# Four of twelve modulation chunks moved from the input projection into the first attention tile, with changes to row loads, hidden turns and the seams

## The chip, the cores and the metric

One core of a Trainium2 chip runs the whole program. The time is the device time of one execution in microseconds (us); the profile is one profiled execution of the same program. Engines: PE (TensorE), DVE (VectorE), ACT (ScalarE), POOL (GpSimd), and SP, which here only issues DMAs.

## The reference, cut to what matters

Two layers of a transformer block over 512 latent tokens and 256 context tokens, width 1024, all in float32. In the second layer only the latent tokens are carried on.

```python
for l in range(2):
    mod   = silu(c)     @ w_mod[l] + b_mod[l]      # (6144,) for the latent stream
    mod_c = silu(c_ctx) @ w_mod[l] + b_mod[l]      # (6144,) for the context stream
    sh1, sc1, g1, sh2, sc2, g2 = split(mod, 6)     # 1024 values each
    h = rms_norm(x, norm_mix) * (1 + sc1) + sh1
    u = h @ w_in[l]                                # 2400 columns: four mixers' q, k, v
    x = x + g1 * (concat(gqa, neighbourhood, diff, mla) @ w_out[l])
    h2 = rms_norm(x, norm_ffn) * (1 + sc2) + sh2
    x = x + g2 * (shared_expert(h2) + routed_experts(h2))   # 16 experts, top 2
out = rms_norm(x, final_norm)
```

The kernel computes `mod` in 12 chunks of 512 columns. Chunks 0 to 3 are sh1 and sc1, 4 and 5 are g1, 6 and 7 sh2, 8 and 9 sc2, 10 and 11 g2.

## The kernel before, in words

Every engine has its own program, written out by hand; semaphores (`s[...]`) tie them together, and each engine runs its instructions strictly in order. SP's program is a queue too: a wait in it holds back every DMA behind it. Each layer has four stages.

**Input projection** (`unit`, L1223 on). 24 units (4 column panels of `w_in` by 6 token tiles) run on PE, and between their halves the small `prep_round` transposes. `mod_product` (L1134) computes one modulation chunk: 32 products into one PSUM bank, of 128 columns each, four to a column group. Its weights are 2 MB, loaded by SP's `mod_load`. `MODS_AT` says behind the first half of which unit chunks 4 to 11 run in layer 0; `MODS_LATE` shifts them by two units in layer 1. DVE adds the bias rows in `mod_row`; `mod_gain` turns sc2 into the gain (chunks 8 and 9); SP's `mod_store` writes chunks 4 to 11 to the DRAM tensor `mod` once all are done.

**Attention**. `NS` = 10 steps for each tile of 128 query tokens, numbered n over all tiles. On PE a step is, in this order: `score` of the step; in the first tile, one or two `nb_unit`s (the last pieces of the projection, steps 0 to 5); the transposes of the step before for the first head (`product(.., 0)`, L1334); the product of an older step with the values (`values`, L1365, "the values between the two groups of transposes"); pieces of the output projection of the tile before (`out_piece`, L1382); and the transposes for the second head (`product(.., 1)`). Step 0 of tile 1 and some later ones use score operands (L1305) that SP has copied from one group of partitions to another: PE stands in `score` at n = 10 for `copies_in`.

After the bias loads SP's queue for the layer reads, in order (L699 to L712): wait for the last `nb_unit`; load `w_out` (4 MB, three DMAs, L700 and L701); load six broadcast vectors g1, sc2, sh2 of both streams from `mod` (0.5 MB each, L704); the eight partition copies (L711, L712); then the row loads and stores of the tiles (`att_rows`). The first of these is x of tile 0 (L722).

**Shared expert and routing**. `hs_load` brings back rows of h2 (L731), `s_turn` (L1440) transposes them, `s_gate`, `s_up`, `s_turn_hid` and `s_down` compute the shared expert, and the router's small products and DVE operations lie between them.

**Routed experts**, then the **seam**: the last block's rows come back through PE (`late_rows`, L1630), DVE adds them (`c_late`, `y_add`), and the next layer's `transpose_x` starts, or, in layer 1, the final norm and the stores.

Of the kernel before, what the change touches and what calls it, by code (L numbers as in the profile page):

```python
# [7 lines left out]
ALU = mybir.AluOpType  # L8
# [46 lines left out]
NB_IN_STEP = {0: [2], 1: [3], 2: [4], 3: [5], 4: [6], 5: [7]}  # L55
# [26 lines left out]
MODS_AT = {3: 4, 5: 5, 7: 6, 9: 7, 11: 8, 13: 9, 15: 10, 17: 11}  # L82
# [100 lines left out]
def program(nc, A, out):  # L183
# [15 lines left out]
    with ExitStack() as ctx:  # L199
# [74 lines left out]
        tmpA, tmpB = take(512), take(512)  # L274
        xt = [take(D) for _ in range(2)]
# [35 lines left out]
        def mod_norm_at(l, half):  # L311
# [13 lines left out]
        PTa, PTb, PTd = take(NTOK), take(NTOK + 2 * P), [take(NTOK), take(NTOK + P)]  # L325
        OT = [take(KT, P) for _ in range(2)]
        dO, dSq = take(P), take(P)
# [34 lines left out]
        mod_w = [[slot[0], slot[2], mod_w2, mod_w3] + [slot[2]] * (NMCH - 4),  # L362
                 mod_late + [slot[1], mod_w5, slot[2], mod_w5, slot[2], mod_w5] + [slot[2]] * (NMCH - 9)]
# [75 lines left out]
        copies_in = sem("copies_in")  # L439

        X_IN = ["x_in0", "x_in1"] + ["x_rest_in"] * (T - 2)
        NAMES = ["mod_w_in0", "mod_w_in1", "mod_w_in2", "mod_w_in3", "mod_w_in4", "mod_rows_in", "mod_mm", "mod_row", "mod_gain", "mod_stored",
# [91 lines left out]
        def nb_bank(n):  # L534

            return ubank[n] if n < NB_AHEAD else B7
# [45 lines left out]
        def _(sp):  # L582
            first = at["ident"][1]
            for l in range(DEPTH):
# [15 lines left out]
                def mod_store(l):  # L600
                    sp.wait_ge(s["mod_gain"], 2 * l + 2)
                    for r in range(2):
                        sp.dma_start(mod_d[l][r, 2 * D:6 * D].rearrange("(n q c) -> q n c", q=4, c=MODQ),
                                     mod_row0[r:P:32, 4:NMCH]).then_inc(s["mod_stored"], 16)
                    sp.wait_ge(s["mod_stored"], 32 * (l + 1))
# [33 lines left out]
                if l == 0:  # L639
# [24 lines left out]
                    for n in range(7, 10):  # L664
                        mod_load(0, n, n)
                    win_load(0, 3, 2 * T)
                    for n in range(10, NMCH):
                        mod_load(0, n, n)
                    win_load(0, 4, 3 * T)
                    mod_store(0)  # L670
                else:
# [5 lines left out]
                    for n in range(6, 9):  # L677
                        mod_load(1, n, n - 1)
                    win_load(1, 3, 2 * T)
                    mod_load(1, 9, 8)  # L680
                    for n in range(10, NMCH):
                        mod_load(1, n, n)
# [8 lines left out]
                for h in range(4):  # L691
                    for r2 in range(2):
# [146 lines left out]
                for t in range(nt):  # L839
# [11 lines left out]
                    if l == 0 and t == T - 1:  # L851

                        sp.wait_ge(late_y, late_tiles[0])
# [9 lines left out]
                for t in range(nt):  # L863
                    sp.wait_ge(s["c_x3"], gc(t) + 1)
                    sp.dma_start(dst(span(t * P, P)), x3[t]).then_inc(s[f"c_stored{t % 2}"], 16)
                for b in range(2):
                    sp.wait_ge(s[f"c_stored{b}"], 16 * (gend // 2))
# [3 lines left out]
        def _(act):  # L871
# [13 lines left out]
            for l in range(DEPTH):  # L885
# [55 lines left out]
                def evac_nb(n):  # L941

                    kind, i, c0, c1 = NB_UNITS[l][n]
                    act.wait_ge(s["u_mm"], UNIT0[l] + NTU + n + 1)
                    if n == 0:

                        act.wait_ge(s["mod_stored"], 32 * (l + 1))
# [185 lines left out]
        def _(pe):  # L1133
            pe.wait_ge(cs_ready, 3)  # L1134
            for l in range(DEPTH):
# [29 lines left out]
                def idle_products():  # L1165
# [1436 lines left out]
```

## Time and profile before

| | us |
|---|---|
| runs before: median, lowest, highest of 3 | 1645.83, 1645.29, 1653.87 |
| the profiled execution's own time | 1647.25 |
| its span in the profile | 1645.1 |
| PE busy in the span | 1572.1 (96%) |
| DVE, ACT, POOL busy | 837.5, 428.8, 196.8 |
| mean granted TensorE clock | 0.989 of full speed |

The span is the time from the first to the last instruction of the profile; 2.15 us of the profiled execution's time lie around it. Rows of the timeline give start, duration, engine, line, operation and count, and in brackets the idle time of the engine just before with what ended it. A float32 product shows as two records on PE, so the 32 products of a modulation chunk stand as x64.

### The profile page before, as it was taken

The numbers are of one execution on the slowest core, as the hardware profiler recorded it, in microseconds if no ns is written. First come the engines' busy times: TensorE is split into PE (matmuls) and PEld (weight loads), VectorE is DVE, ScalarE is ACT, GpSimd is POOL, SyncE is SP. The second block draws the span as 40 slices with busy tenths as digits, with TensorE's granted clock in tenths as the row PEclk, the third lists the DMA queues.
The fourth block names the chain that finished last, engine by engine and source line by source line (L and its number), as shares of the span: only waits on it lengthen the run. The fifth ranks groups of instructions, "written<-read, shape, count | busy, mean of one in ns | idle before, by whom it ended". The sixth has DMA issues, their size and how long they took to land.

```text
span 1645.1 us, 26409 instructions
## 1 busy us (share of the span) xinstructions
PE 1572.1 (96%) x10090; PEld 1054.5 (64%) x10090; DVE 837.5 (51%) x1791; ACT 428.8 (26%) x922; POOL 196.8 (12%) x348
## 2 busy tenths in 40 slices
PE   6999999899999989999999999999899999999996
PEld 4655445666665567788888555555666666688873
DVE  2222534567665657555555721434667665644345
ACT  1322113455454410000000312113455541000001
POOL 0110102000000000222221110202000000021212
PEclk9999999999999999999999999999999999999998
DMA  9764230600001286689888774331501016478885
GB/s 354 235 236 154 103 45 7 202 1 32 22 26 39 94 300 255 211 319 335 329 323 305 260 257 154 130 65 36 178 1 40 14 61 224 182 277 315 311 319 193
DMA packets 113425, 285.60 MB, mean 174 GB/s; under 512 B 32945, under 2 KB 42863, under 8 KB 103535
## 3 DMA queue, kind: packets, MB, share of 16 engines
q1 hardware_dynamic: 101942, 263.13, 46.1%
q0 software_dynamic: 10800, 20.99, 3.4%
q8 instruction: 66, 1.08, 0.3%
q14 instruction: 33, 0.26, 0.1%
q10 hardware_dynamic: 584, 0.14, 0.0%
HBM read 265.47 MB, written 40.37 MB: 186 GB/s over the span
## 4 chain that ended last, share of the span: by engine, by line
PE 82%; DMA 6%; SPq 5%; DVE 3%; issue 2%; ACT 1%; POOL 0%; POOLq 0%; DVEq 0%; ACTq 0%
PE S L1577 15%; PE S L1238 14%; PE S L1317 7%; PE B L1382 7%; PE S L1588 7%; PE B L1365 6%; PE PT L1334 5%; PE B L1257 3%; PE B L1144 2%; PE PT L1512 2%; DMA arena<-in_w_mod 2%; PE S L1257 2%; PE S L1448 1%; DMA arena<-in_moe_w_up 1%; PE PT L1472 1%
## 5 line engine op out<-in xcount | busy, mean ns | idle before, releaser
L1238 PE MATMUL S<-arena 128*128 128x512 f32 (+3 forms) x768 | 300.2, 541 | 3.8 <-ACT arena L903 3.8
L1577 PEld LDWEIGHTS S<-arena 128*128 128x128 f32 x2304 | 263.6, 192 | 19.4 <-issue 19.3
L1577 PE MATMUL S<-arena 128*128 128x128 f32 x2304 | 265.3, 275 | 1.4 <-DMA arena<-in_moe_w_up 0.9
L1238 PEld LDWEIGHTS S<-arena 128*128 128x128 f32 x768 | 141.8, 193 | 125.4 <-issue 105.2
L1009 ACT ACTIVATE arena<-S,nmax 128x768 f32<-128x768 f32 (+1 forms) x200 | 161.9, 813 | 163.8 <-DVE nmax L2062 120.6
L2062 DVE TENSOR_REDUCE nmax<-S 128x1 f32<-128x768 f32 (+1 forms) x168 | 133.1, 825 | 75.7 <-PE S L1317 65.6
L1382 PE MATMUL B<-arena 128*128 128x512 f32 x320 | 156.5, 613 | 1.9 <-DVE arena L2116 1.9
L1334 PEld LDWEIGHTS PT<-cst,arena 128*128 128x128 f32 x832 | 94.6, 141 | 84.6 <-issue 57.4
L1317 PE MATMUL S<-arena 64*128 64x256 f32 (+5 forms) x624 | 144.7, 504 | 4.1 <-ACT arena L1009 2.4
L1334 PE MATMUL PT<-cst,arena 128*128 128x128 f32 x832 | 121.4, 278 | 19.0 <-issue 11.3
L1588 PE MATMUL S<-arena 128*128 128x512 f32 x288 | 129.6, 593 | 1.2 <-DVE arena L2195 1.2
L1028 ACT ACTIVATE arena<-PT 128x768 f32<-128x768 f32 (+3 forms) x100 | 81.1, 811 | 117.7 <-PE PT L1337 58.6
L1365 PE MATMUL B<-arena 128*64 128x128 f32 x1664 | 109.3, 279 | 2.5 <-issue 2.4
L1317 PEld LDWEIGHTS S<-arena 64*128 64x128 f32 (+2 forms) x624 | 67.5, 189 | 59.3 <-issue 53.0
L1365 PEld LDWEIGHTS B<-arena 128*64 128x64 f32 x1664 | 90.3, 137 | 23.1 <-issue 23.1
L1061 ACT ACTIVATE arena<-S 128x256 f32<-128x256 f32 x36 | 13.8, 384 | 346.9 <-PE S L1577 346.9
L2209 DVE COPY arena<-PT 128x512 f32<-128x512 f32 x36 | 24.9, 691 | 136.6 <-PE PT L1512 136.6
L1382 PEld LDWEIGHTS B<-arena 128*128 128x128 f32 x320 | 54.4, 189 | 53.1 <-issue 48.8
L1588 PEld LDWEIGHTS S<-arena 128*128 128x128 f32 x288 | 52.0, 191 | 54.2 <-issue 54.2
L2177 DVE RECIPROCAL arena<-arena 128x256 f32<-128x256 f32 x46 | 80.6, 1753 | 1.6
L1876 DVE TENSOR_TENSOR arena<-B,arena 128x128 f32<-128x128 f32 x24 | 7.0, 290 | 132.2 <-PE B L1144 116.8
L2088 DVE COPY arena<-PT 128x768 f32<-128x768 f32 (+1 forms) x60 | 50.6, 844 | 36.8 <-PE B L1365 22.5
(321 smaller groups left out, 1775.1 us busy)
## 6 DMA issues: line engine op xcount, KB each, us to landing
arena<-in_w_mod SPq DMA_DIRECT2D x24, 2048.0 KB, 11.3
arena<-in_moe_w_gate SPq DMA_DIRECT2D x36, 1024.0 KB, 6.4
arena<-in_moe_w_up SPq DMA_DIRECT2D x36, 1024.0 KB, 9.5
arena<-in_moe_w_down SPq DMA_DIRECT2D x36, 1024.0 KB, 6.8
arena<-in_w_in SPq DMA_DIRECT2D x6, 2048.0 KB, 11.5
arena<-y SPq DMA_DIRECT2D x20, 512.0 KB, 5.9
arena<-mod SPq DMA_DIRECT2D x16, 512.0 KB, 16.6
arena<-in_tokens SPq DMA_DIRECT2D x12, 512.0 KB, 10.3
```

The lines of the kernel that those rows point to most:

```text
L1009: act.activation(p_buffer(k, m)[:, 0:nk], (S0, S1)[m][:, 0:nk], ACT.Exp, bias=nmax[:, 2 * k + m:2 * k + m + 1], accum_out=rsum[:, 2 * k + ...
L1028: act.activation(t_buffer(k, 1)[:, 0:width], PT[:, 0:width], ACT.Copy).then_inc(s["pt_s"], 1)
L1238: mm = pe.matmul(ubank[u % 4][:, c0:PANEL_W[p]], hT[:, k, t * P:(t + 1) * P], panel[p][:, k, c0:], start=k == 0, stop=k == KT - 1)
L1257: mm = pe.matmul(nb_bank(n)[:, 0:c1 - c0], panel[4][:, k, w0:w0 + P], hT[:, k, c0:c1], start=k == 0, stop=k == KT - 1)
L1317: mm = pe.matmul((S0, S1)[m][:, c0:c1], qk[rows, qs, cols], qk[rows, ks, NTOK - nk + c0:NTOK - nk + c1], start=True, stop=True)
L1334: tr = pe.transpose(PT[:, c0:c0 + P], p_buffer(k, m)[:, c0:c0 + P], ident)
L1365: mm = pe.matmul(B6[64 * m:64 * m + 64, 0:P], vals[:, (NTOK - nk) // P + j, v0 + 64 * m:v0 + 64 * m + 64], bufs[m][:, j * P:j * P + P], st ...
L1382: mm = pe.matmul(B7[:, :], OT[t % 2][:, j, :], wout[:, j, c * 512:(c + 1) * 512], start=at_ == 0, stop=at_ == KT - 1)
L1577: mm = pe.matmul(to, wgu[b][:, w, k * DE + h * P:k * DE + (h + 1) * P], XT[b][:, k, :], start=k == 0, stop=k == KT - 1)
L1588: mm = pe.matmul((S0, S1)[b][:, c * 512:(c + 1) * 512], hid[b][:, k * P:(k + 1) * P], wdn[b][:, k, c * 512:(c + 1) * 512], start=k == 0, s ...
L2062: dve.tensor_reduce(nmax[:, 2 * k + m:2 * k + m + 1], Sm[:, 0:nk], AX.X, ALU.max, negate=True).then_inc(s["neg_max"], 1)
L2177: ch.done(dve.reciprocal(gx, gx)).sync()
```

## The change

1. Chunks 8 to 11 leave the projection. `MODS_AT` becomes units 3, 6, 9, 12 for chunks 4 to 7. The four others run in tile 0 of attention, in steps 4, 6, 7 and 9 (`FAR_STEPS`), between `values` and the second group of transposes, into the bank B7. Their rows live in a buffer of their own (`far_row`), filled by two DVE copies.
2. SP's queue changes with it. `mod_store` writes only chunks 4 to 7. Chunk 9's weights are loaded when chunk 8's product is done; chunk 10's behind the last `nb_unit`; then half of `w_out`; chunk 11's when chunk 9's product is done; then SP waits for all twelve products, loads the other half of `w_out`, and in `far_store` stores chunks 8 to 11 and waits until they are in DRAM. The six vector loads and the eight partition copies stand behind that, in their old order.
3. In layer 0 the last two `nb_unit`s move together into step 5.
4. The first two `hs_load`s move one tile earlier and ahead of the shared expert's weights. The hidden turns and the routing's order change (`route_blocks` ahead of `s_out`, a turn before the wait for the counts; in layer 1 `s_down(2)` ahead of the routing table).
5. Seams: 6 and 7 idle products ahead of layer 1's first transposes and first unit; `c_late` waits for half a row at a time; the `y_add`s move behind the last `e_up_mul`; the final norm's order changes and the last tile is stored in two halves.

```diff
-NB_IN_STEP = {0: [2], 1: [3], 2: [4], 3: [5], 4: [6], 5: [7]}
+NB_IN_STEP = {0: [2], 1: [3], 2: [4], 3: [5], 5: [6, 7]}
-MODS_AT = {3: 4, 5: 5, 7: 6, 9: 7, 11: 8, 13: 9, 15: 10, 17: 11}
+MODS_AT = {3: 4, 6: 5, 9: 6, 12: 7}
+FAR = 8
+FAR_STEPS = {4: 8, 6: 9, 7: 10, 9: 11}
...
                 def mod_store(l):
+                    sp.wait_ge(s["mod_row"], NMCH * l + FAR)
+                    for r in range(2):
+                        sp.dma_start(mod_d[l][r, 2 * D:4 * D].rearrange("(n q c) -> q n c", q=4, c=MODQ),
+                                     mod_row0[r:P:32, 4:FAR]).then_inc(s["mod_stored"], 16)
+                    sp.wait_ge(s["mod_stored"], 64 * l + 32)
+
+                def far_store(l):
+
+                    sp.wait_ge(s["mod_row"], NMCH * (l + 1))
                     sp.wait_ge(s["mod_gain"], 2 * l + 2)
                     for r in range(2):
...
+                        sp.dma_start(mod_d[l][r, 4 * D:6 * D].rearrange("(n q c) -> q n c", q=4, c=MODQ),
+                                     far_row[r:P:32]).then_inc(s["mod_stored"], 16)
+                    sp.wait_ge(s["mod_stored"], 64 * (l + 1))
...
+                mod_load(l, 9, 9)
                 sp.wait_ge(s["u_mm"], UNIT0[l + 1])
+                mod_load(l, 10, 0)
                 for kv in range(2):
...
-                sp.dma_start(wout[:, 2:KT, :], A["w_out"][l][2 * P:D, :].rearrange("(k p) n -> p k n", p=P)).then_inc(s["wout_in"], 16)
+                sp.dma_start(wout[:, 2:4, :], A["w_out"][l][2 * P:4 * P, :].rearrange("(k p) n -> p k n", p=P)).then_inc(s["wout_in"], 16)
+                mod_load(l, 11, 10)
+                sp.wait_ge(s["mod_mm"], NMCH * (l + 1))
+                sp.dma_start(wout[:, 4:KT, :], A["w_out"][l][4 * P:D, :].rearrange("(k p) n -> p k n", p=P)).then_inc(wout_late_in, 16)
+                far_store(l)
                 for stream in range(2):
                     for n, w in enumerate((2, 4, 3)):
                         sp.dma_start(vec[:, 3 * stream + n, :], mod_d[l][stream, w * D:(w + 1) * D].partition_broadcast(P))
...
                 def s_weights():
                     sp.wait_ge(s["scored"], 2 * NS * gend)
+                    for b in range(2):
+                        hs_load(b)
...
                 def s_first_loads():
-                    for b in range(2):
-                        hs_load(b)
                     sp.wait_ge(s["pv_done"], NJ * gend)
...
+                    if l and u == 0:
+                        idle_products(7)
...
+                if l:
+                    idle_products(6)
                 transpose_x(0)
...
+                    if t == 0 and c == 0 and j >= 4:
+                        pe.wait_ge(wout_late_in, 16 * (l + 1))
...
                     for piece in pieces:
                         out_piece(t - 1, piece)
+                    if n in FAR_STEPS:
+
+                        pe.wait_ge(s["u_evac"], min(UNIT0[l] + NTU + 6, UNIT0[l + 1]) if n < 5 else UNIT0[l + 1])
+                        pe.wait_ge(s["mod_row"], NMCH * l + FAR_STEPS[n])
+                        mod_product(l, FAR_STEPS[n], B7)
                     if after:
                         product(tp, kp, 1)
...
+                    if n in FAR_STEPS:
+                        mod_row(l, FAR_STEPS[n], B7[:, :])
+                        if FAR_STEPS[n] == NMCH - 1:
+                            mod_gain(l, 1)
...
                 def c_late(t):
-                    dve.wait_ge(late_y, late_tiles[0] * l + t + 1)
                     for c in range(2):
+                        dve.wait_ge(late_y, 2 * (late_tiles[0] * l + t) + c + 1)
```

## Rows read from the trace of the kernel before

**Rows 1.** The page's first part: busy time, share, instructions.
```profile
PE 1572.1 (96%) x10090; PEld 1054.5 (64%) x10090; DVE 837.5 (51%) x1791; ACT 428.8 (26%) x922; POOL 196.8 (12%) x348
```

**Rows 2.** Timeline of PE, layer 0, projection: start, us, line, count.
```profile
56.83 1.95 PE L1144 MATMUL B<-arena,cs 128*32 128x128 f32 x64
...
70.45 1.95 PE L1144 MATMUL B<-arena,cs 128*32 128x128 f32 x64 [1.13 <-DMA arena<-in_w_mod]
```

**Rows 3.** Timeline of PE, layer 1, projection.
```profile
965.14 1.95 PE L1144 MATMUL B<-arena,cs 128*32 128x128 f32 x64 [0.63 <-DMA arena<-in_w_mod]
...
1056.71 1.95 PE L1144 MATMUL B<-arena,cs 128*32 128x128 f32 x64 [0.75 <-DMA arena<-in_w_mod]
```

**Rows 4.** Timeline of PE, layer 0, attention: tile 0's end, tile 1's start.
```profile
304.49 1.04 PE L1334 MATMUL PT<-cst,arena 128*128 128x128 f32 x6 [2.01 <-ACT arena L1009]
...
312.56 1.56 PE L1317 MATMUL S<-arena 64*128 64x512 f32 x8 [1.60 <-ACT arena L1009]
...
324.11 0.85 PE L1334 MATMUL PT<-cst,arena 128*128 128x128 f32 x6 [1.18 <-issue]
...
326.00 0.70 PE L1305 MATMUL S<-arena 32*128 32x512 f32 x2 [0.94 <-DMA arena<-arena]
```

**Rows 5.** Timeline of PE, layer 1, tile 0 of attention.
```profile
1162.28 1.51 PE L1334 MATMUL PT<-cst,arena 128*128 128x128 f32 x6 [2.02 <-ACT arena L1009]
...
1182.40 0.85 PE L1334 MATMUL PT<-cst,arena 128*128 128x128 f32 x6 [1.18 <-issue]
```

**Rows 6.** Timeline of SP, layer 0: issue start, time to issue, count.
```profile
299.25 0.60 SPq L701 DMA_DIRECT2D arena<-in_w_out  x1
299.89 6.68 SPq L704 DMA_DIRECT2D arena<-mod  x6
306.67 1.19 SPq L711 DMA_DIRECT2D arena<-arena  x1
```

**Rows 7.** The chain that ended last, stretch 296 to 330 us.
```profile
312.75 13.01 DMA arena<-arena
```

**Rows 8.** DMA issues: count, KB each, us to landing; page, then three short stretches.
```profile
arena<-in_w_out SPq DMA_DIRECT2D x2, 3072.0 KB, 15.4
...
arena<-in_w_mod SPq DMA_DIRECT2D x1, 2048.0 KB, 10.0
...
x_mix<-arena SPq DMA_DIRECT2D x1, 512.0 KB, 17.2
...
h<-arena SPq DMA_DIRECT2D x1, 512.0 KB, 2.7
```

**Rows 9.** Timeline, layer 0, attention's end to routing, PE and DVE.
```profile
592.16 1.97 PE L1440 MATMUL PT<-cst,arena 128*128 128x128 f32 x8 [2.55 <-DMA arena<-h]
...
594.17 0.69 DVE L2170 COPY arena<-PT 128x512 f32<-128x512 f32 x1 [2.50 <-PE PT L1440]
...
638.97 1.96 PE L1144 MATMUL B<-arena,cs 128*32 128x128 f32 x64 [1.30 <-DVEq L2273]
```

**Rows 10.** Timeline of PE, layer 1, the routing table.
```profile
1421.98 1.94 PE L1491 MATMUL B<-arena 128*128 128x24 f32 x16 [0.87 <-DVEq L2327]
```

**Rows 11.** Windows: stretch, length, PE and others busy, PEclk, DMA share, GB/s.
```profile
1163.00:1166.00 3.00, 3.00 (x11) 1.64 (x11) 0.94 (x2) 0.92 (x1) 0.00 (x0) 0.50 1.02 406
921.00:924.00 3.00, 3.00 (x6) 1.75 (x6) 2.39 (x3) 0.57 (x1) 0.00 (x0) 0.50 1.02 416
```

**Rows 12.** Timeline of PE: idle products in layer 0, layer 1's first work.
```profile
19.47 3.40 PE L1168 MATMUL S<-cs 128*32 128x256 f32 x15
...
917.96 1.09 PE L1162 MATMUL PT<-cst,arena 128*128 128x128 f32 x8 [2.04 <-DVE arena L1857]
920.71 5.06 PE L1238 MATMUL S<-arena 128*128 128x352 f32 x8 [1.66 <-ACT arena L903]
```

**Rows 13.** Timeline of PE, layer 1, the last expert block.
```profile
1618.49 3.67 PE L1588 MATMUL S<-arena 128*128 128x512 f32 x8 [1.21 <-DVE arena L2195]
```

More of the change, by code:

```diff
@@ L274, in program @@
         tmpA, tmpB = take(512), take(512)
+        XT_START = take.at[0]
         xt = [take(D) for _ in range(2)]
@@ L325, in program @@
         PTa, PTb, PTd = take(NTOK), take(NTOK + 2 * P), [take(NTOK), take(NTOK + P)]
+        OT_START = take.at[0]
         OT = [take(KT, P) for _ in range(2)]
+        assert OT_START + KT * P >= XT_START and OT_START + 2 * KT * P <= XT_START + 2 * D
+        far_row, far_norm = OT[1][:, 0:4, :], OT[1][:, 4:6, :]
         dO, dSq = take(P), take(P)
@@ L534, in nb_bank @@
         def nb_bank(n):
-            return ubank[n] if n < NB_AHEAD else B7
+            return ubank[n] if n < NB_AHEAD else B7[:, 256 * (n % 2):256 * (n % 2) + 256] if n >= 6 else B7
         def nb_units_in(l, n):
@@ L663, in _ @@
                     sp.dma_start(rel_copies, rel_d[0].partition_broadcast(GRID_W)).then_inc(rel_step, 16)
-                    for n in range(7, 10):
-                        mod_load(0, n, n)
+                    mod_load(0, 7, 7)
                     win_load(0, 3, 2 * T)
-                    for n in range(10, NMCH):
-                        mod_load(0, n, n)
+                    mod_load(0, 8, 8)
                     win_load(0, 4, 3 * T)
@@ L676, in _ @@
                     win_load(1, 2, T)
-                    for n in range(6, 9):
+                    for n in range(6, 8):
                         mod_load(1, n, n - 1)
                     win_load(1, 3, 2 * T)
-                    mod_load(1, 9, 8)
-                    for n in range(10, NMCH):
-                        mod_load(1, n, n)
+                    mod_load(1, 8, 8)
                     win_load(1, 4, 3 * T)
@@ L863, in _ @@
                 for t in range(nt):
-                    sp.wait_ge(s["c_x3"], gc(t) + 1)
-                    sp.dma_start(dst(span(t * P, P)), x3[t]).then_inc(s[f"c_stored{t % 2}"], 16)
+                    parts = [(0, 512), (512, D)] if l and t == nt - 1 else [(0, D)]
+                    for n, (c0, c1) in enumerate(parts):
+                        sp.wait_ge(s["c_x3"], gc(t) + 1 + n)
+                        sp.dma_start(dst(span(t * P, P))[:, c0:c1], x3[t][:, c0:c1]).then_inc(s[f"c_stored{t % 2}"], 16)
                 for b in range(2):
-                    sp.wait_ge(s[f"c_stored{b}"], 16 * (gend // 2))
+                    sp.wait_ge(s[f"c_stored{b}"], 16 * (gend // 2 + l * b))
         @block.scalar
@@ L1163, in transpose_x, with idle_products @@
                     tr.then_inc(s["hT_tr"], 1)
-                def idle_products():
-                    for _ in range(8):
+                def idle_products(n=8):
+                    for _ in range(n):
                         pe.matmul(S1[0:32, 0:32 * KT], cs[:, 0, :], cs.rearrange("p k x -> p (k x)"), start=True, stop=True)
@@ L1557, in _ @@
                     route_counts()
-                    s_down(0)
-                    s_turn_hid(1)
-                    s_down(1)
-                    s_turn_hid(2)
+                    for t in range(2):
+                        pe.wait_ge(s["s_hts"], g(t) + 1)
+                        s_turn_hid(t + 1)
+                        s_down(t)
                     s_up(3)
+                    s_down(2)
                     pe.wait_ge(s["r_took"], 2)
                     route_table()
-                    pe.wait_ge(s["s_hts"], g(2) + 1)
                     s_turn_hid(3)
-                    s_down(2)
                     s_down(3)
@@ L2069, in out_heads @@
                     dve.wait_ge(s["pt_s"], s_evacs(l, t, k) + 1)
+                    if t == 1 and JOB_NO[job] == 0:
+                        dve.wait_ge(s["mod_stored"], 64 * (l + 1))
                     if t >= 2:
@@ L2394, in _ @@
                             x_half(0, 0)
[L2395 removed]
                         if t == 0:
                             route_blocks()
+                        s_out(t)
                         if t == 0:
@@ L2416, in _ @@
                     route_slots()
+                    s_out(0)
                     route_blocks_hot()
@@ L2447, in e_out, with e_block @@
                                              ALU.mult, ALU.mult).then_inc(s["e_y"], 1)
-                def e_block(blk, u, b, more, first, out_first, meanwhile=None):
+                def e_block(blk, u, b, more, first, out_first):
                     last = not first or b
```

76 lines of the change are left out of this document (39 added, 37 removed).

## The prediction, made before the run

> **What bounds the kernel now.** I read the page's busy shares first: PE is busy 96% of the span [rows 1], so anything that only moves PE work is worth nothing, and only PE's waits, its slow-clock stretches and its order against SP's queue can pay or cost. Then I read PE's timeline in the stages that the change touches. In the projection PE has almost no holes: one wait for chunk weights in layer 0 [rows 2] and two in layer 1 [rows 3]. In tile 0 of attention there are a few waits of 1 to 2 us, for ScalarE's exponentials or PE's own issue [rows 4, 5]. Last I read SP's queue and the chain that ended last in the stretch around tile 1's start. There the chain isn't PE's: it runs through SP's issues of `w_out`, the vectors and the partition copies, and PE stands 0.94 us at L1305 for the last copy [rows 4, 6, 7]. In layer 0 these copies are already just late. That is the row on which the forecast hangs.
>
> **Projection.** Eight chunk products leave it, four in each layer, of 1.95 us each [rows 2]: 15.6 us. The waits for chunk weights go too, since chunks now have three units between them instead of two: 1.13 us [rows 2] and 0.63 + 0.75 us [rows 3], 2.5 us in all.
>
> **Tile 0 of attention.** The eight products come back, +15.6 us. Where PE waits for another engine right behind the new place, the product covers the wait. Layer 0: step 6 has a wait of 2.01 (the product covers 1.95), step 7's product stands ahead of the wait of 1.60, step 9's ahead of 1.18 [rows 4]: 4.7 us. Layer 1: 1.95 of the 2.02, and 1.18 [rows 5]: 3.1 us. Step 4 has no wait to cover. In layer 1 PE ran three microseconds at the lower level (granted 0.50, 1.2 GHz) right behind that wait of 2.02 [rows 11]; with the hole filled I take back half of them, 1.5 us. Against this, chunk 9's weights are requested only when chunk 8's product is done, and one such load alone took 10.0 us [rows 8]. Two steps of attention are about as long (in layer 0 there are two projection units between as well, so nothing). For layer 1 I take 1.3 us of waiting. Bounds of this paragraph's net beyond the 15.6: -9.3 (no wait for weights) to +6 (nothing covered, and chunks 9 and 11 each 3 us late in one layer). I take -4.7 - 3.1 - 1.5 + 1.3 = -8.0, since every wait named stands directly behind a new product.
>
> **The copies.** This is the large term. In the new queue, `w_out`'s second half, the store of chunks 8 to 11, the vectors and the copies all stand behind chunk 11's product, which is in step 9, the last of tile 0. PE needs the copies in step 0 of tile 1. Count from E, the end of chunk 11's product:
> - Half of `w_out`, 2 MB, is issued at once. A 2 MB load alone lands after 10.0 us [rows 8]: E + 10.1.
> - The store is issued about 1 us later (DVE must first add the rows and make the gain) and SP waits for its landing. With nothing ahead, a store of h2 landed in 2.7 us; with modulation weights ahead of it, one took 17.2 us [rows 8]. So a store waits for the large load ahead of it: E + 10.4.
> - Six vectors and eight copies. Before, their issuing ran from 299.89 to about 313.3 (the last one starts at 312.75 and takes about as long as the 0.6 of the other single ones), 13.4 us, and the last copy landed at 312.75 + 13.01 = 325.76 [rows 6, 7]. `w_out` was ahead of them and landed at 299.25 + 15.4 = 314.65 [rows 6, 8], so their own 3.5 MB took the 11.1 us behind it. With the queue empty the last copy lands between 2 + 11.1 = 13.1 us (data sets it) and 13.4 + 2.7 = 16.1 us (issue sets it) after the first vector. I take 15: E + 25.
>
> PE has one group of transposes left behind E (0.85 us for six [rows 4], with the seventh 1.1) and then stands still: 24 us in each layer. Nothing can cover it, because PE runs in order: scores of tile 1 are behind the wait, and so everything on DVE and ACT that feeds on them. Two layers less the 0.94 that was there [rows 4]: +47.1 us. PE then wakes at the lower clock. After a hole of 2 to 4 us the trace shows 3 us windows at 0.50 [rows 11], which cost 1.5 us and their flanks some more; I take 2 us a layer, +4. Sum of the term: +51.
>
> Its bounds: if the store is not held by `w_out`, the data are still there: 10.1 + 11.1 = E + 21, 20 us a layer, 40 with the clock at nothing. If the last copy takes its 13.01 us again behind 13.4 us of issue [rows 6, 7], it lands at E + 36.8: 35.7 a layer, 75 with the clock. I stay near the low end, because those 13 us were a backlog that is now gone.
>
> The Trainium skill, "DMA: Bandwidth & Descriptors", section "Queues, rings and completion order", says that a DMA's semaphore write lands only after every earlier write of the same DMA engine, so that completion is not in order over all engines but a small store can't finish ahead of a big load on the engines that both use. The 17.2 us agree. Without this rule the term would be its low bound, 40, with it 51. [...]
>
> **Attention to routing.** In layer 0 the rows of h2 arrive 2.55 us late for PE [rows 9]; now they are requested a tile earlier and are no limit. DVE sat idle 2.50 us before it took the first turned row [rows 9] and can't start sooner than that hole, so the gain is 2.5 us (bounds 0, if the g2 vectors then end last, and 4, with the turns at the full clock). In layer 1 the DVE is busy up to the turn, and I take nothing. With `route_blocks` ahead of `s_out` the wait of 1.30 us before the next chunk product goes [rows 9]. In layer 1 the table's wait of 0.87 us goes [rows 10], but `s_down(2)` now stands ahead of the table, which makes the token list and the first gather about 2 us later; PE can end up waiting for it. I take +0.5 (bounds -0.9 and +2). Together -3.3.
>
> **Seam between the layers.** 15 records of idle products took 3.40 us [rows 12], two records being one product, so 13 products take about 5.7 us, in holes of 2.04 and 1.66 us [rows 12]: PE starts its first unit 2.0 us later. In return the first half unit doesn't run at 0.50 [rows 11, 12]: 5.06 us against about 2.5. The half-row waits bring DVE 0.4 us. Net -1.0 (bounds +2, if the clock falls anyway, and -2.5).
>
> **End.** The wait of 1.21 us at the last block [rows 13] goes, because `y_add` no longer stands ahead of `e_up_mul`. The other changes of the final norm I count at nothing: I take -1.2 (bounds 0 and -2.5).
>
> **Sum.** -2.5 - 8.0 + 51 - 3.3 - 1.0 - 1.2 = +35.0 us (the 15.6 out and the 15.6 back in cancel). Against the profiled execution's 1647.25, whose span is 1645.1 with 2.15 us around it, that is 1682.3; the median of the runs shown is 1.4 us lower, and from it I forecast 1645.8 + 35 = **1681 us**.
>
> **The rivals.**
> - *The copies are hidden anyway.* They land within 1.1 us of E, or something ahead of them isn't waited for. Then only the gains are left: -16.0, 1630 us. It decides below about 8 us of standing still for each layer: 16 us of gains against two stalls. For it: the small terms are real waits. Against it: the issue of 14 DMAs alone took 13.4 us [rows 6, 7], and the wait for the store comes on top. This is the case on the other side.
> - *Long landing.* The copies queue behind the vectors as before and land 13 us after their issue [rows 7]. 35.7 us a layer, +75 in place of +51: 1705 us.
> - *Starved chunks.* Chunk 9 and, behind 2 MB of `w_out`, chunk 11 each come late in both layers, since each load waits for an earlier product. At 2 MB in 10.0 us [rows 8], with 4 MB ahead of the last, up to 4 us a chunk: +16 less what I counted (1.3): 1696 us.
> - *Short stall.* The store isn't held by `w_out` and only data set the end: 40 for 51: 1670 us.
>
> **How the numbers follow.** Forecast 0.6; copies hidden 0.04; long landing 0.1; starved chunks 0.13; short stall 0.13. The forecast's own spread is that of 13.1 to 16.1 us in two layers and of the small terms, some 6 us to either side. The range that leaves no more than 2 in 10 out reaches from below the short stall, with the gains a little larger, to the starved chunks: 1663 to 1698 us. About 0.5%, 8 us, is what a measurement of this kernel can tell from no change. Only the first case ends below that: faster 0.04; a mixture of it with a short stall could end near zero: same 0.02; slower 0.94.
>
> **What would show it.** Right: in both layers L1305 at n = 10 waits for the DMA of the partition copies, 20 to 27 us, with PE, DVE and ACT empty; L704 issues some 10 us behind chunk 11's product; granted clock 0.5 in the first microseconds after. PE's waits for modulation weights in the projection gone; those of 2.01, 1.60 and 2.02 us in tile 0 gone or below 0.5. L1440 without a wait for h in layer 0. Wrong: if L1305 shows no wait above 8 us, the queue's order is not what holds PE; if a wait for modulation weights above 3 us stands in steps 6 to 9, the chunks are the limit; if the stall is right and the total isn't, a seam or the routing has a new wait, the first gather of layer 1 ahead of all.

## The result, and the profile after

The change makes the kernel slower: 1689.17 us median (1688.68 to 1689.81, 4 runs) against 1646.30 (1645.29 to 1653.87, 4 runs) for the kernel before on the same chip, a ratio of 1.0247 with an interval of 1.0223 to 1.0271. The forecast was 1681 us, in a range of 1663 to 1698.

The page of the profile after: the first part, then two lines of the 40 slices of 42 us.

```profile
PE 1571.8 (93%) x10116; PEld 1056.7 (63%) x10116; DVE 840.7 (50%) x1796; ACT 429.1 (25%) x922; POOL 196.2 (12%) x348
...
PE   6999999499999989999999999999399998999996
...
PEclk9999999799999999999999999999799999999998
```

PE does the same work as before, 1571.8 us against 1572.1 [rows 1], in a span of 1688.0 instead of 1645.1: 42.9 us were added in which it stands still. Two slices show where, one in each layer, and in both the granted clock falls too. The waits of PE name them (total, times, longest):

```profile
PE S L1333 <- DMA arena<-arena: 48.9, 2, 25.1
PE B L1166 <- DMA arena<-in_w_mod: 13.1, 4, 10.5
...
PE S L1618 <- DMA arena<-in_moe_w_up: 7.7, 7, 2.8
PE B L1412 <- DVE arena L2164: 4.0, 2, 3.1
```

L1333 is the line that was L1305 in [rows 4], the scores that read the partition copies. The first line alone is the forecast stall, 48.9 us in two waits where 48 were expected. The 10.5 us of the second are the first chunk of layer 0, at the start of the program, where the profile before waits 10.3. PE in layer 0, around chunk 11 (L1166) and tile 1's first scores, answers to [rows 4]:

```profile
312.86 1.96 PE L1166 MATMUL B<-arena,cs 128*32 128x128 f32 x64
314.75 0.87 PE L1362 MATMUL PT<-cst,arena 128*128 128x128 f32 x6
315.46 0.27 PE L1365 MATMUL PT<-cst,arena 128*128 128x128 f32 x1
340.82 1.22 PE L1333 MATMUL S<-arena 32*128 32x512 f32 x2 [25.09 <-DMA arena<-arena]
```

Behind the product come seven transposes, then nothing for 25.09 us. Layer 1 has the same picture (23.81 us), and two short waits for chunk weights:

```profile
1176.02 1.95 PE L1166 MATMUL B<-arena,cs 128*32 128x128 f32 x64 [1.33 <-DMA arena<-in_w_mod]
...
1182.89 1.96 PE L1166 MATMUL B<-arena,cs 128*32 128x128 f32 x64 [1.05 <-DMA arena<-in_w_mod]
...
1222.69 1.22 PE L1333 MATMUL S<-arena 32*128 32x512 f32 x2 [23.81 <-DMA arena<-arena]
```

SP's queue over the same stretch of layer 0, answering to [rows 6]: the late half of `w_out` (L720), the store (L621), the vectors (L724), and the first and last partition copy (L731, L732).

```profile
314.88 0.38 SPq L720 DMA_DIRECT2D arena<-in_w_out  x1
315.58 1.16 SPq L621 DMA_DIRECT2D mod<-arena  x2
322.99 3.72 SPq L724 DMA_DIRECT2D arena<-mod  x6
326.81 0.62 SPq L731 DMA_DIRECT2D arena<-arena  x1
...
331.64 0.78 SPq L732 DMA_DIRECT2D arena<-arena  x1
```

And the chain that ended last (start, us, what), answering to [rows 7]:

```profile
312.93 1.93 PE B L1166 x64
314.88 0.29 DVE arena L1918
315.17 0.34 DVE arena L1925
315.58 0.57 SPq L621
316.20 6.77 DMA mod<-arena
...
331.64 8.93 DMA arena<-arena
...
340.82 0.80 PE S L1333
```

From E = 314.8, the end of chunk 11's product, the chain runs product, row add, gain, store, vectors, copies, scores: the chain of the prediction, step for step. Two windows of the same stretch (bounds, length, busy time of PE, PEld, DVE, ACT and POOL, granted clock, DMA share and GB/s), the wait and the first microseconds behind it:

```profile
325.00:341.00 16.00, 0.18 (x3) 0.21 (x6) 0.00 (x0) 0.00 (x0) 0.00 (x0) 0.50 0.88 234
341.00:345.00 4.00, 4.00 (x19) 2.83 (x21) 1.82 (x2) 1.04 (x3) 0.00 (x0) 0.50 0.00 0
```

The engines are empty, but for the 0.18 us of PE at the very end, and only the DMA works. The first 4 us of PE's work behind it run at the lower level (granted 0.50, 1.2 GHz).

**Where the 42.9 us are.** Each row is a stretch between two first products on PE, in us against the profile before; the expert loop of layer 0 ends where its last down product starts, and the seam starts there. The last row of a column is the difference of the spans. "Copies early" and "move alone" are the first and the ninth of the experiments below.

| stretch on PE | forecast | after | copies early | move alone |
|---|---|---|---|---|
| L0 projection, start to first score | -8.9 | -10.7 | -10.7 | -9.3 |
| L0 tile 0, to the first score of tile 1 | +26.2 | +25.5 | +0.7 | +0.9 |
| L0 attention, to the first shared gate product | -0.5 | +2.7 | +1.0 | -0.5 |
| L0 routing, to the first expert product | -1.3 | -1.6 | -1.6 | +0.9 |
| L0 expert loop | 0 | +7.1 | +5.1 | +6.8 |
| seam and L1 projection | -10.2 | -9.8 | -9.8 | -10.2 |
| L1 tile 0 | +28.5 | +26.3 | +2.6 | +2.0 |
| L1 attention | +2.0 | +2.9 | -0.1 | 0.0 |
| L1 routing | +0.5 | -0.8 | -0.8 | -0.1 |
| L1 expert loop and end | -1.2 | +1.4 | +3.3 | -1.5 |
| span | +35 | +42.9 | -10.3 | -11.0 |

### The profile page after: what moved, and what is told of

The parts are those of the page before. It is cut to its first block, busy times and chain, and to the rows that moved or that the text cites. A ratio compares the mean times of both kernels' runs of the same rounds, so it can differ in the third digit from the quotient of the medians.

```text
span 1688.0 us, 26488 instructions
## 1 busy us (share of the span) xinstructions
PE 1571.8 (93%) x10116; PEld 1056.7 (63%) x10116; DVE 840.7 (50%) x1796; ACT 429.1 (25%) x922; POOL 196.2 (12%) x348
## 4 chain that ended last, share of the span: by engine, by line
PE 78%; DMA 9%; DVE 5%; SPq 2%; issue 2%; ACT 1%; POOL 0%; DVEq 0%; POOLq 0%; ACTq 0%
PE S L1262 16%; PE S L1618 12%; PE B L1412 8%; PE S L1345 7%; PE S L1629 6%; PE B L1393 5%; PE PT L1362 5%; DMA arena<-in_moe_w_up 5%; PE B L1283 3%; PE B L1166 2%; PE S L1283 2%; DMA arena<-in_w_mod 2%; PE PT L1548 2%; PE PT L1508 1%; PE S L1491 1%
## 5 line engine op out<-in xcount | busy, mean ns | idle before, releaser
L1262 PE MATMUL S<-arena 128*128 128x512 f32 (+3 forms) x768 | 296.3, 536 | 2.2 <-ACT arena L925 2.2
L1618 PEld LDWEIGHTS S<-arena 128*128 128x128 f32 x2304 | 265.5, 193 | 25.5 <-issue 25.4
L2136 DVE COPY arena<-PT 128x768 f32<-128x768 f32 (+1 forms) x60 | 50.6, 844 | 37.3 <-PE B L1393 25.5
L1768 POOL TENSOR_TENSOR drs<-dvar,halfs 128x2 f32<-128x2 f32 x20 | 14.0, 700 | 471.6 <-DVE dvar L2096 471.6
## 6 DMA issues: line engine op xcount, KB each, us to landing
arena<-in_w_mod SPq DMA_DIRECT2D x24, 2048.0 KB, 10.5
```

Of the source, the lines that this page charges most:

```text
L1262: mm = pe.matmul(ubank[u % 4][:, c0:PANEL_W[p]], hT[:, k, t * P:(t + 1) * P], panel[p][:, k, c0:], start=k == 0, stop=k == KT - 1)
L1618: mm = pe.matmul(to, wgu[b][:, w, k * DE + h * P:k * DE + (h + 1) * P], XT[b][:, k, :], start=k == 0, stop=k == KT - 1)
```

## The experiments

The main theory is the forecast's: PE waits for the copies because everything ahead of them in SP's queue stands behind chunk 11. Its rivals: the stall is the price of filling tile 0 with products, whatever the queue does; or the vectors or the late `w_out`, once moved, turn into a wait of their own. For the small edits: the row loads gain 2.5 us, or they lose. Experiments 1 to 4, 5 to 8 and 9 to 10 each ran on one chip, where the kernel before had medians of 1650.96, 1650.36 and 1650.72 us. A ratio is always against that.

**1. The copies early (`e1_copies_early`).** The eight copies are issued right behind the bias loads and ahead of chunk 9's load. All else is as in the change.

```diff
                         sp.dma_start(dst.rearrange("p (j c) -> p j c", c=GRID_W), src).then_inc(s["bias_in"], 16)
+                wait_all_rounds(sp, l)
+                for i in (0, 2):
+                    for m in range(2):
+                        rows, to = slice(32 * m, 32 * m + 32), SL_MK + i + m
+                        sp.dma_start(qk[96:P, to, 0:SEQ], qk[rows, SL_DQ + i // 2, 0:SEQ]).then_inc(copies_in, 16)
+                        sp.dma_start(qk[96:P, to, SEQ:NTOK], qk[rows, SL_DK + i // 2, SEQ:NTOK]).then_inc(copies_in, 16)
                 mod_load(l, 9, 9)
```

> The changed kernel with one edit: SP issues the eight partition copies right behind the bias loads, ahead of chunk 9's weights, so behind none of the twelve products. Theory A (SP's order is the whole stall): the waits of 25.1 and 23.8 us at the first score of tile 1 are gone and so are the slow microseconds behind them; 48.9 + about 4 off 1689.2 gives 1636 us, with the vectors landing before step 16 needs them. Rival B (something else behind the twelve products holds PE next, the vectors in step 16 or the late half of w_out in step 12): PE stands there instead, 1660 us or more. Rival C for the expert loops: their four longer waits for in_moe_w_up in layer 0 (6.3 us against 0.7 before) come from where in time the loop starts; then they change here too, to as little as 1630 us; if they come from the code they stay.

Measured: 1636.88 us (1636.24 to 1639.52, 6 runs), ratio 0.9923 (0.9896 to 0.9950). Same layer, same place on PE:

```profile
313.27 1.96 PE L1166 MATMUL B<-arena,cs 128*32 128x128 f32 x64
315.15 0.88 PE L1362 MATMUL PT<-cst,arena 128*128 128x128 f32 x6
315.87 0.27 PE L1365 MATMUL PT<-cst,arena 128*128 128x128 f32 x1
316.07 0.70 PE L1333 MATMUL S<-arena 32*128 32x512 f32 x2
```

Only the order of SP's queue differs, and the hole is gone; the first score now takes 0.70 us instead of 1.22. The span shrinks from 1688.0 to 1634.8, 53.2 us, of which 48.4 lie in the two tile 0 stretches of the table and 4.7 in the attention behind them. The stall is the queue's, and the products in tile 0 cost 0.7 and 2.6 us for the 15.6 that the projection loses. No other wait comes in its place.

**2. The copies ahead of the vectors (`e2_copies_before_vec`).** They still stand behind the late `w_out` and the store.

```diff
                 far_store(l)
+                wait_all_rounds(sp, l)
+                for i in (0, 2):
...
                 for stream in range(2):
```

> The changed kernel with the eight copies between far_store and the six vector loads; they still wait for all twelve products and the store. Theory A: the copies no longer wait for 3.7 us of vector issues and 3 MB of vector data; their own eight issues take 5.6 us and the last lands about 3 us later, so at E + 8.2 + 8.6 = E + 17 where the trace has E + 25.8: 9 us less in each layer, 1671 us. Rival (the end is set by the store and by a fixed landing time of these small copies, 8 to 9 us each whatever is ahead): the last lands at E + 8.2 + 5.6 + 8.5 = E + 22.3, 3.5 us less in each layer, 1682 us.

Measured: 1673.43 us (1671.26 to 1676.55, 4 runs), ratio 1.0136 (1.0097 to 1.0174). The wait at L1333:

```profile
PE S L1333 <- DMA arena<-arena: 27.5, 2, 13.8
```

The last copy in the chain of layer 0:

```profile
328.32 1.93 DMA arena<-arena
```

The vectors ahead of the copies were worth 11.3 us in layer 0 (25.09 less 13.84) and 21.4 over both. Without them the last copy lands 1.93 us after its issue instead of 8.93, so the rival of a fixed landing time of 8 to 9 us is out, and the wait is shorter than even the theory had it (E + 14.5, not E + 17).

**3. The late `w_out` behind the copies (`e3_wout_behind`).**

```diff
                 sp.wait_ge(s["mod_mm"], NMCH * (l + 1))
-                sp.dma_start(wout[:, 4:KT, :], A["w_out"][l][4 * P:D, :].rearrange("(k p) n -> p k n", p=P)).then_inc(wout_late_in, 16)
                 far_store(l)
...
+                sp.dma_start(wout[:, 4:KT, :], A["w_out"][l][4 * P:D, :].rearrange("(k p) n -> p k n", p=P)).then_inc(wout_late_in, 16)
```

> The changed kernel with the late half of w_out issued behind the copies, so nothing large is ahead of far_store's store. Theory A (the store was held behind the 2 MB load): the store lands about 2.7 us after its issue in place of 6.8, the copies as much earlier, 4.1 us in each layer, 1681 us. Rival (a store of this shape takes its 6.8 us anyway, or the data behind it set the end): 1687 to 1689 us.

Measured: 1679.06 us (1678.14 to 1680.52, 4 runs), ratio 1.0174 (1.0136 to 1.0213). SP in layer 0:

```profile
315.74 1.15 SPq L621 DMA_DIRECT2D mod<-arena  x2
318.09 3.67 SPq L723 DMA_DIRECT2D arena<-mod  x6
```

With nothing large ahead, SP is past the store 2.35 us after its first issue. In the change it was past it after 322.99 - 315.58 = 7.41 us. The two waits at L1333 fall to 19.97 and 20.08 us, 8.8 us less together, and nothing waits for the late `w_out`. If the gains of experiments 2 and 3 add up, which was not run, the stall of layer 0 splits into 5.1 us for the store behind `w_out`, 11.3 for the vectors, and the rest, some 9, for the copies' own issue and landing and for the store itself.

**4. The row loads back (`e4_rows_back`).** Experiment 1 with the two `hs_load`s where they stood before.

```diff
                     sp.wait_ge(s["scored"], 2 * NS * gend)
-                    for b in range(2):
-                        hs_load(b)
...
                 def s_first_loads():
+                    for b in range(2):
+                        hs_load(b)
```

> The kernel of e1_copies_early with the two early row loads of h2 (hs_load) put back where they were, behind the next tile's x load. The prediction's step: the row loads gain 2.5 us in layer 0, so this kernel is 2.5 us slower than e1. Theory D, from the trace of the changed kernel (SP issues 5.3 us of shared weights later, so the store of x_mix lands late, DVE waits 2.15 us for it and PE 3.12 in place of 1.06 us, then 1.6 us of slow clock): the early row loads cost about 3 us net, so this kernel is 3 us faster than e1.

Measured: 1635.63 us (1630.96 to 1640.83, 6 runs), ratio 0.9906 (0.9877 to 0.9936). That is 1.3 us below experiment 1, inside both intervals, so the total shows no gain of the early loads, and can't rule out one of 2.5 us. The profile after, where the loads are early, shows what they push back. SP in layer 0:

```profile
584.30 0.83 SPq L751 DMA_DIRECT2D arena<-h  x2
...
587.39 4.03 SPq L763 DMA_DIRECT2D arena<-in_shared_w_down  x1
591.46 1.35 SPq L746 DMA_DIRECT2D x_mix<-arena  x1
```

With the two row loads ahead of it, the last of the shared weights takes 4.03 us to issue instead of 2.14 in the profile before, and the store of x_mix behind it lands 9.07 us after its issue, against 6.2 in experiment 4. In experiment 1 the store isn't even issued later than in experiment 4 (248.3 us behind tile 1's first score in both), but it lands after 9.54 us; so it is at least as much the loads in front of it that hold it as the later issue. DVE waits for that store to land before it overwrites the row, and PE waits for DVE. The first row is DVE's, the others are PE's:

```profile
600.56 0.69 DVE L2164 TENSOR_TENSOR arena<-B,arena 128x512 f32<-128x512 f32 x1 [2.15 <-DMA x_mix<-arena]
```

```profile
601.30 8.69 PE L1412 MATMUL B<-arena 128*128 128x512 f32 x16 [3.12 <-DVE arena L2164]
...
612.91 3.91 PE L1484 MATMUL B<-arena 128*128 128x272 f32 x16 [1.12 <-DVE arena L2222]
```

The wait for h of [rows 9] is gone, as forecast; one of 3.12 us stands ahead of the last out-projection, where the profile of experiment 4 has 1.05. What was saved behind was lost in front: from tile 1's first score to the first expert product experiment 4 takes 351.3 us and experiments 1, 7 and 8, with the loads early, 352.2, 350.5 and 350.4.

**5. The row loads early in the kernel before (`e5_before_rows`).** The edit of experiment 4, the other way round, in the old kernel.

> The kernel before with one edit: the two early row loads (hs_load) moved as in the change, ahead of the shared weights of the last tile but one. The prediction's step: 2.5 us faster. Theory D (the later x_mix store makes DVE and PE wait): PE's wait at L1382 ahead of the last output projections grows from 1.06 to 2.4 to 3.1 us and some slow clock follows, the wait of 2.55 us at the turn goes; from the kernels run so far, first shared gate at +1.5 us and the turn's start of the experts 0.7 us shorter: 0.8 us slower, within the noise. It is also a second profile of the old code's expert loop: theory C-code (the loop in layer 0 is longer by the code changed) wants 227.5 us again from the first expert product to the last down product; theory C-noise wants any value between 227 and 241.

Measured: 1651.77 us (1647.16 to 1659.73, 10 runs), ratio 1.0008 (0.9988 to 1.0028): nothing, and the forecast gain of 2.5 us (a ratio of 0.9985) lies just outside the interval. Its profile gave something else. The expert loop of layer 0, whose code is here the old one, took 240.5 us against 227.5 in the profile before. PE's waits for expert weights in both layers, profile before and then this one:

```profile
PE S L1577 <- DMA arena<-in_moe_w_up: 0.9, 2, 0.7
```

```profile
PE S L1577 <- DMA arena<-in_moe_w_up: 10.7, 8, 2.7
```

So the +7.1 us of that stretch in the table need no cause in the change. In the eleven other profiles the loop took 230 to 241 us, old loop code (experiments 5 and 9: 240.5 and 234.3) or new. The profile before is the shortest, and the one with hardly a wait.

**6. The row loads in a third place (`e6_rows_mid`).** Experiment 1 with the two loads right behind the x_mix store of the last tile but one, so that the shared weights and that store keep their old times.

```diff
                     sp.dma_start(x_mix[l][rows, :], xb).then_inc(s["x1_stored"], 16)
+                    if behind:
+                        behind()
                     sp.wait_ge(s["h2_ready"], g(t) + 1)
```

> The kernel of e1_copies_early with the two early row loads issued directly behind the x_mix store of the last tile but one, so neither ahead of that store nor behind the last x load. Theory D: both waits go, the 3.12 us at the last output projections back to 1.05 and the 2.3 to 2.5 at the first turn to 0; the stretch from tile 1's start to the first shared gate is 2.5 us shorter than with the loads back (268.8) and 4 us shorter than in e1 (270.3): 266.3, in all 1633 us. Rival (the first turned row waits for DVE's sum anyway): 268.5, in all 1635.5.

Measured: 1634.09 us (1631.95 to 1636.61, 4 runs), ratio 0.9901 (0.9884 to 0.9917). PE has neither the wait of 3.12 us nor the one for h:

```profile
578.64 1.05 PE L1476 MATMUL PT<-cst,arena 128*128 128x128 f32 x8
...
581.73 3.90 PE L1484 MATMUL B<-arena 128*128 128x272 f32 x16 [1.13 <-DVE arena L2222]
```

Tile 1's first score to the first gate product takes 266.6 us, here and again in experiment 10, against 268.6 to 270.3 in experiments 1, 4, 7, 8 and 9, with the loads early or late. Two profiles thus have the 2 us that the forecast wanted, in this place; the run times scatter too much to show them.

**7. The old order of the last sums (`e7_tail_back`).** Experiment 1 with the final `y_add`s, `c_late`s and POOL's sum in the order before.

> The kernel of e1_copies_early with the last layer's final order put back: POOL's addition for the last tile ahead of its loop, DVE's c_late, y_add and c_final in the old order (last_out and the two half stores stay new). Theory F (the new order makes DVE's y_add and POOL's addition, both from and to SBUF, run at the same time, 3.25 us in place of 1.2, and puts c_final(0) behind c_late(3), on which POOL's next factors wait): the stretch from the last down product to the end falls from 28.5 to about 25.5 us, 1634 us. Rival (the 2.8 us come from the half stores or from last_out): stays at 28 us or more.

Measured: 1640.27 us (1630.70 to 1643.64, 10 runs), ratio 0.9932 (0.9912 to 0.9952). The end is no shorter: from the start of the last down product to the end of the span it is 28.9 us, against 28.5 in experiment 1 and in the change. The rival of this run's expectation, that the stretch stays at 28 us or more, came true. That doesn't clear the order of the sums, though. DVE's add of 3.25 us (last section) is gone, but in this profile the rows of y land late:

```profile
1616.84 1.23 DVE L2537 TENSOR_TENSOR arena<-arena 128x1024 f32<-128x1024 f32 x1 [2.50 <-DMA arena<-y]
```

SP issued their load 5.3 us ahead of the last down product here and 8.0 us ahead of it in experiment 1.

**8. Without the idle products (`e8_no_idle`).** Experiment 1 without the 6 and 7 idle products of layer 1.

> The kernel of e1_copies_early without the 13 idle products at the start of layer 1. The prediction's step: PE starts its first unit 2.0 us sooner, but at the lower clock level, and loses 2.5 us there: last down product to first unit 14.4 in place of 16.4 us, first unit to first attention score 184.4 in place of 182.0; in all 0.4 us slower than e1. Rival (the idle products are pure loss because the clock would have stayed up): 182.0 stays and the kernel is 2 us faster.

Measured: 1634.23 us (1630.88 to 1639.13, 4 runs), ratio 0.9916 (0.9893 to 0.9938). The seam in experiment 8:

```profile
898.08 3.60 PE L1625 MATMUL S<-arena 128*128 128x512 f32 x8
...
909.29 1.09 PE L1184 MATMUL PT<-cst,arena 128*128 128x128 f32 x8 [1.61 <-DVE arena L1895]
912.04 4.26 PE L1260 MATMUL S<-arena 128*128 128x352 f32 x8 [1.65 <-ACT arena L925]
```

and in experiment 1, which has them:

```profile
900.83 3.60 PE L1629 MATMUL S<-arena 128*128 128x512 f32 x8
...
910.36 2.78 PE L1190 MATMUL S<-cs 128*32 128x256 f32 x12
913.07 1.09 PE L1184 MATMUL PT<-cst,arena 128*128 128x128 f32 x8
914.10 3.21 PE L1190 MATMUL S<-cs 128*32 128x256 f32 x14
917.23 2.63 PE L1262 MATMUL S<-arena 128*128 128x352 f32 x8
```

The first half unit gains 1.6 us from them (2.63 against 4.26), but 2.78 + 3.21 us of idle products fill holes of only 1.61 + 1.65. The first unit starts 16.4 us behind the start of the last down product with them (the first row of each fence) and 14.0 without. From that same start to layer 1's first score it is 198.4 us with them, in every profile that has them, and 197.6 without: they lose 0.8 us. Experiment 10, which leaves them out too, has 198.7 for the same stretch, so their net is nothing that these profiles can tell.

**9. The move alone (`e9_chunks_alone`).** The kernel before with points 1 to 3 of the change and the copies early; row loads, turns, seam and end as before.

> The kernel before with the chunk move alone: four chunks of each layer in tile 0, copies right behind the bias loads, late w_out and norm-row store as in the change; row loads, turns, seam and tail stay as before. Theory A (the move gives what the starts of the two stretches show in the run with early copies, -9 to -10 us a layer up to the first out-projection, less 1 to 3 us in tile 0, and the other edits together give nothing): about 1632 us, ratio 0.990 to 0.993, the same as the run with early copies within 3 us. Theory B (the other edits give the 5.5 us that the prediction gave them): about 1642 us, ratio 0.995 to 0.998, 5 us above that run.

Measured: 1635.36 us (1629.05 to 1642.37, 6 runs), ratio 0.9902 (0.9866 to 0.9938). The other edits together give nothing that can be measured in the time. The stretches say that this nothing is a gain and a loss. The routing of layer 0 takes 81.8 us in the kernels with the new order of turns (82.6 in experiment 4, with the rows back), against 83.4, 84.3 and 83.5 in the three with the old order (the profile before, experiments 9 and 5). From the start of the last down product to the end it is the other way round: 26.6, 25.7 and 25.8 us with the old end, 27.5 to 29.0 in the nine profiles with the new one.

**10. What the experiments point to (`e10_best`).** Experiment 1 with the edits of 6 and 8.

> The changed kernel with the copies right behind the bias loads, the two row loads right behind the x_mix store of the last tile but one, and without the 13 idle products of layer 1. If the two gains add up (2 to 4 us from the row loads, 2.6 us from the idle products, both seen in profiles), 1631 us, ratio 0.988. If both were scatter between executions, 1636 to 1637, ratio 0.992.

Measured: 1631.62 us (1630.24 to 1640.86, 6 runs), ratio 0.9900 (0.9865 to 0.9936), the lowest median of all kernels here and with 1628.4 us the shortest profiled span. That it beats the kernel before is shown. That it beats experiments 6, 8 and 9 isn't: the intervals overlap. The 2.6 us that its expectation gives to the idle products are not in the traces (experiment 8).

## Why the prediction was right

**The stall: mechanism and size right, two of its terms off in opposite directions.** The forecast was E + 25 and 24 us of waiting a layer; measured were E + 25.8 and 25.09, 23.81. The store let SP go at E + 8.2, not E + 10.4, because the 2 MB of `w_out` landed in 8.0 us instead of the 10.0 of the nearest row [rows 8]. In return the vectors and copies took 340.57 - 322.99 = 17.6 us instead of 15, outside the bounds of 13.1 and 16.1 given for them: the last copy, small as it is, landed 8.9 us after its issue, where I had taken a store's 2.7, in a stretch where the DMA moved 234 GB/s. Issue alone took 9.4 us (322.99 to 332.42) where I had 13.4 from a queue with a backlog, so the data set the end, not the issue; experiment 2, with no vectors ahead and 1.93 us of landing, bears this out. Why the data took longer than the 11.1 us read from the profile before isn't shown. That the two errors, 2.2 us too much and 2.6 too little, cancel is luck, and so is a stall within 1 us of 24. The clock behind the stall cost 4.7 us in both layers (attention stretches of the table, after less copies early), forecast 4. The whole term: 53.2 us by experiment 1 against 51.

**The store did wait for the load.** Experiment 3 shows it: 7.41 us with the load ahead, 2.35 without. The rival of the short stall fell with it. The Trainium skill, "DMA: Bandwidth & Descriptors", section "Queues, rings and completion order", says that a semaphore write lands only after every earlier write of the same DMA engine. The two times agree; whether it is this rule that holds the store or simply its place in the queues behind the load, no run here tells apart. Long landing and starved chunks fell too: 25.8 instead of 36.8, and waits for chunk weights of 1.33 and 1.05 us in layer 1 and 0.22 in layer 0, 2.6 in all for the 1.3 taken.

**Projection and tile 0: better than forecast.** Projection is -9.3 in layer 0 and -10.2 in layer 1 in experiment 9, which has the old seam (forecast -8.9 and, without the seam's -1.0, -9.2). In tile 0 the forecast left +2.2 and +4.5 us without the stall (3.1 less the 0.94; 7.8 - 3.1 - 1.5 + 1.3), and experiment 1 has +0.7 and +2.6. The holes were about as forecast: besides the 0.94, PE's idle time in tile 0 falls by 4.3 us in layer 0 (forecast 4.7) and by 1.9 in layer 1 (3.1 less the 1.3 of waiting for weights). The difference is the clock. For 7.8 us of products PE is busy only 6.0 and 4.6 us longer, with the granted clock up from 0.98 to 1.00 and from 0.95 to 1.00: read as clock, some 1.8 and 3.2 us came back where I had 0 and 1.5.

**Row loads: the step that failed.** "The gain is 2.5 us", with bounds of 0 to 4, looked at the wait that goes and not at what the two loads push back in SP's queue. The x_mix store lands later, and DVE and PE wait for it; experiments 4 and 5 show a net of nothing, and the profiles of experiments 6 and 10 some 2 us once the loads stand behind that store.

**Seam and end.** The parts of the seam came out near their sizes, those of the idle products a little worse. They make the first unit start 2.4 us later (forecast 2.0) and give back 1.6 us of clock (2.5); the half-row waits shorten the first hole from 2.04 to 1.61 us (0.4). Net, the new seam is 0.4 us longer than the old one of experiment 9 (198.4 against 198.0), where I had -1.0.

The end is the other step that failed. The wait of 1.21 us [rows 13] is gone in the change, but it is not there in experiments 5 and 9 either, which have the old order: I had taken a wait of one profile for one of the code. And the changes of the final norm, which I counted at nothing, go with an end that is 1 to 3 us longer (experiment 9). In the change and in experiments 1, 4 and 10, 2.0 us of it are DVE's add that takes 3.25 us in place of 1.21; in the five others DVE waits there for the rows of y or for POOL's sum. Which edit is to blame was not separated. In layer 1 the wait of 0.87 us [rows 10] goes and one of 1.77 comes at the first expert turn, in line with the forecast's "PE can end up waiting for it", yet the stretch is 0.8 us shorter, not 0.5 longer.

**The difference to the forecast.** By the table it is mostly the expert loop of layer 0 (+7.1), which took 13 us longer in experiment 5 without any change to it. The ratios leave that one profile out: the change costs 0.0247 x 1646.3 = 40.7 us, experiment 1 gains 0.0077 x 1651 = 12.7, and their difference, 53.4, is the 53.2 of the spans. Against the forecast's +35 that is 5.7 us more: 2 from the stall (53 for 51), and some 3.5 from the small terms, which gave 12.7 where I had 16. The interval of experiment 1's gain reaches from 8 to 17 us, so this second part is not measured by the times. Its stretches, without that loop, say how the small terms missed: the row loads by 3.5 us and the end by 4.5 to the bad, layer 0's projection by 1.8, the two tiles 0 by 3.4 and layer 1's routing by 1.3 to the good.

## What to carry to other kernels

Before work is moved to a later place, list what the issuing queue holds behind it: here four cheap products took a store, six loads and eight copies with them, and the last of these was already 0.94 us late. The products were worth having (1635 us with the copies issued more than 80 us earlier, against 1651), so the remedy is the queue's order, not the old place. A load requested earlier delays every store that stands behind it, and an engine may be waiting for that store. And before a stretch of some us is put down to a change, look at how far it scatters under the old code: one profile of before was at the edge of what that loop does, and one of its waits, the 1.21 us at the end, was missing in the two others with the same code there.

## What the runs showed of the hardware

**DVE and POOL adding in SBUF at the same time.** Near the end of the change's layer 1, DVE and then POOL, each adding two rows of SBUF:

```profile
1667.35 1.21 DVE L2538 TENSOR_TENSOR arena<-arena 128x1024 f32<-128x1024 f32 x1
...
1669.71 3.25 DVE L2538 TENSOR_TENSOR arena<-arena 128x1024 f32<-128x1024 f32 x1
```

```profile
1669.52 2.35 POOL L1866 TENSOR_TENSOR arena<-arena 128x1024 f32<-128x1024 f32 x1
```

The same DVE add takes 1.21 us alone and 3.25 when POOL's began 0.19 us before it: about its own time behind the end of POOL's (1669.52 + 2.35 + 1.21 = 1673.08, measured 1672.96). Experiment 1 has the same 3.25 beside the same 2.35. In experiment 3 POOL began its add 0.51 us behind DVE's start, and there DVE took 1.22 and POOL 2.91 in place of 2.35. The Trainium skill, "SBUF — State Buffer", section "SBUF: two separate sides", says that such a pair of operations doesn't share bandwidth: the one that starts first holds the pair of ports they share for its whole instruction and the other waits. The rows agree, in both orders.

**Small copies behind large loads.** Partition copies of 32 and 64 KB inside SBUF took 8.1 to 8.6 us (medians of the two sizes in the two layers), and the last of layer 0 8.9 us, from issue to landing when 3 MB of vectors had been issued ahead of them, although they have no part in that data. With the copies ahead of the vectors (experiment 2) the last one took 1.93 us in layer 0 and 1.89 in layer 1.
